# Moving the shared expert's first product into the second layer's routing stage, and slot 4's loads and the shared second product one step earlier

## The reference, cut to what matters

```
scores = sigmoid(h @ w_router)                 # 64 experts
... 8 experts of 64 per token, with gates      # group-limited top-k
routed = sum_e gate_e * (silu(h @ w_gate[e]) * (h @ w_up[e])) @ w_down[e]
shared = (silu(h @ sh_gate) * (h @ sh_up)) @ sh_down      # every token
h = layer_norm(ALPHA * h + routed + shared)
```

## Time and profile before

| | |
|---|---|
| median of 3 runs | 1616.32 us (1610.67 to 1619.49) |
| span of the profiled execution, first to last instruction | 1614.9 us |
| PE busy | 1455.4 us (90%) |
| DVE busy | 689.6 us (43%) |
| ACT busy | 355.2 us (22%) |
| POOL busy | 250.1 us (15%) |
| moved by DMA | 512.46 MB, mean 317 GB/s |
| mean granted clock of PE | 0.952 |

### The profile page before, as it was taken

How to read it: one execution, slowest core, us unless ns; L and a number is a source line. 1 busy time by engine, 2 the same in 40 slices (tenths; PEclk the granted TensorE clock), 3 DMA queues, 4 the chain that set the end, 5 groups by cost and what they waited for, 6 DMA issues and landing times. The chain is left out here.

```text
span 1614.9 us, 24656 instructions
## 1 busy us (share of the span) xinstructions
PE 1455.4 (90%) x9414; PEld 859.4 (53%) x9414; DVE 689.6 (43%) x1471; ACT 355.2 (22%) x744; POOL 250.1 (15%) x323
## 2 busy tenths in 40 slices
PE   8999888998888999797999878986999997979996
PEld 6788667887534545343454456873434342424442
DVE  3888747732433434333343349043233342323324
ACT  3766454220411111011111030122001111111111
POOL 5779515200100000000000000001000000000000
PEclk9999999899899999998999988897999998989999
DMA  7679361011999999999999973295999999999994
GB/s 272 207 190 241 137 169 54 2 53 60 393 416 420 426 422 424 423 423 424 420 425 421 406 268 110 98 401 191 362 425 424 422 425 426 422 423 422 426 423 195
DMA packets 101490, 512.46 MB, mean 317 GB/s; under 512 B 36836, under 2 KB 42020, under 8 KB 66300
## 3 DMA queue, kind: packets, MB, share of 16 engines
q1 hardware_dynamic: 91548, 481.81, 75.0%
q0 software_dynamic: 9824, 29.05, 4.7%
HBM read 508.92 MB, written 17.10 MB: 326 GB/s over the span
## 5 line engine op out<-in xcount | busy, mean ns | idle before, releaser
L1731 PE MATMUL banks<-experts,e_xgT 128*64 128x512 f32 (+1 forms) x1408 | 306.4, 608 | 1.2 <-issue 1.2
L1943 DVE TENSOR_TENSOR e_ac<-e_sl,banks 128x256 f32<-128x256 f32 x54 | 22.7, 421 | 408.3 <-ACT e_sl L1852 408.3
L280 PE MATMUL banks<-hT,dense_ring 128*128 128x272 f32 x768 | 185.4, 400 | 5.0 <-DMA dense_ring<-in_w_in 4.9
L1334 POOL DMA_INDIRECT x_xg<-rows_dram,x_idx x54 | 53.5, 991 | 853.6 <-DVE x_idx L1326 836.2
L1731 PE MATMUL banks<-dense_ring,e_xgT 128*64 128x512 f32 (+1 forms) x320 | 148.6, 619 | 39.5 <-issue 38.2
L1731 PEld LDWEIGHTS banks<-experts,e_xgT 128*64 128x64 f32 (+1 forms) x1408 | 102.4, 132 | 150.6 <-issue 150.6
L280 PEld LDWEIGHTS banks<-hT,dense_ring 128*128 128x128 f32 x768 | 147.1, 193 | 39.9 <-DMA dense_ring<-in_w_in 5.4
L1782 PE MATMUL banks<-experts,e_aT 128*64 128x512 f32 (+1 forms) x704 | 156.3, 606 | 6.2 <-DVE hT L1905 4.3
L1731 PEld LDWEIGHTS banks<-dense_ring,e_xgT 128*64 128x64 f32 (+1 forms) x320 | 41.0, 130 | 134.8 <-issue 132.7
L1852 ACT ACTIVATE e_sl<-banks 128x256 f32<-128x256 f32 x54 | 20.8, 385 | 402.3 <-PE banks L1731 402.3
L1749 PE MATMUL banks<-x_sg,e_ys 128*128 128x272 f32 x432 | 104.5, 394 | 2.8 <-ACT e_ys L1867 1.4
(11 more groups left out here) (444 smaller groups left out, 2072.6 us busy)
## 6 DMA issues: line engine op xcount, KB each, us to landing
experts<-in_moe_gate_up SPq DMA_DIRECT2D x88, 2048.0 KB, 26.8
experts<-in_moe_down SPq DMA_DIRECT2D x88, 1024.0 KB, 26.3
dense_ring<-in_moe_gate_up SPq DMA_DIRECT2D x20, 2048.0 KB, 15.2
dense_ring<-in_moe_down SPq DMA_DIRECT2D x40, 1024.0 KB, 25.2
dense_ring<-in_w_in SPq DMA_DIRECT2D x47, 512.0 KB, 4.6
e_gate_up<-in_moe_gate_up SPq DMA_DIRECT2D x10, 2048.0 KB, 19.5
x_gate_up<-in_moe_gate_up SPq DMA_DIRECT2D x10, 2048.0 KB, 19.1
dense_ring<-in_w_out SPq DMA_DIRECT2D x4, 2048.0 KB, 8.1
```

What stands on the lines that cost most here:

```text
L280: mm = pe.matmul(ps[g % 4][:, 0:T], slot[:, n % SLOTS_IN, c, :], hT[:, c, :], start=(c == 0), stop=(c == DC - 1))
L1334: pool.indirect_dma_start(out=ex["xg"][:, i % 2, :], out_offset=None, in_=mem["rows_dram"], in_offset=bass.IndirectOffsetOnAxis(ap=ex["idx ...
L1731: mm = pe.matmul(gub[e * n:(e + 1) * n, :], xgT[:, i % 2, c, e * n:(e + 1) * n], gate_up_weights(mem, j)[:, c, :], start=(c == 0), stop=(c ...
L1943: dve.tensor_tensor(ac[:], sl[:], gub[:, FF:], ALU.mult).then_inc(mul, 1)
```

## The change

`halves_ahead` goes away. In layer 1 all four halves of the shared first product, both `silu` and both products with them run in `norm_and_route`, as they already did in layer 0. SP requests slot 4's gate/up half as the first load of the expert stage in both layers (in layer 0 it was that already). In both layers `begin` moves from unit 1 to unit 0, `shared_down` and `add_shared` move from unit 2 to unit 1, and slot 4's down half is requested after them, in unit 1.

```diff
--- before.py
+++ after.py
@@ -1247,12 +1247,6 @@
     return ex
 
 
-def halves_ahead(layer):
-
-
-    return 1 if layer == DEPTH - 1 else 2 * FC
-
-
 def shared_half(pe, mem, ex, hN, bank, j, cs=range(DC)):
 
 
@@ -1370,7 +1364,7 @@
         sort = mem["sort_par"]
         key_off, number, ranks, twice, extras = (sort[:, a:b] for a, b in (
             (0, 1), (1, 2), (2, 2 + E), (2 + E, 2 + E + P), (2 + E + P, 2 + 2 * E + P)))
-        ahead, warm = halves_ahead(layer), sb("warm", [1, 1])
+        warm = sb("warm", [1, 1])
         loaded, gu_ready = mem["router_loaded"], mem["shared_gate_up_ready"]
         meaned, centred, squared, sq_summed, sd_ready, rooted, scaled, out = (sem(n) for n in (
             "meaned", "centred", "squared", "sq_summed", "deviation", "rooted", "scaled", "normed"))
@@ -1472,7 +1466,7 @@
                 pe.matmul(sort_ps[0:1, 0:E], number, at_rank[:], start=True, stop=True)
                 pe.matmul(sort_ps[0:1, E:2 * E], cm[:], at_rank[:], start=True, stop=True).then_inc(sorted_, 1)
                 shared_half(pe, mem, ex, hN, sh_ps[0], 0, range(4, DC))
-                for j in range(1, ahead):
+                for j in range(1, 2 * FC):
                     if j == 3:
                         pe.wait_ge(maxed, 1)
                     shared_half(pe, mem, ex, hN, sh_ps[j], j)
@@ -1509,7 +1503,7 @@
                 act.copy(pg[E:, 0:W], both_ps[E:, 0:W]).then_inc(placed, 1)
                 for i in range(2):
                     gates_in(act, ex, i, spread_ps[i], W)
-                for m in range(min(ahead, FC)):
+                for m in range(FC):
                     shared_silu(act, mem, ex, sh_ps, m, W)
 
             @block.vector
@@ -1605,7 +1599,7 @@
                 dve.wait_ge(ex["rows_broadcast"], 2)
                 link(dve.scalar_tensor_tensor(out=pg[0:E, 0:W], in0=maskT[:], scalar=extra[:, 0:1], in1=pg[0:E, 0:W],
                                               op0=ALU.mult, op1=ALU.add))
-                for m in range(ahead - FC):
+                for m in range(FC):
                     shared_gate(dve, mem, ex, sh_ps, m, W)
 
 
@@ -1643,8 +1637,6 @@
         summed, begun = sem("columns_summed"), sem("sums_begun")
 
 
-        sh_ps, ahead = (None, bank[7], y0b, y1b), halves_ahead(layer)
-
         spread_to = lambda i: (y0b, y1b) if i < AHEAD else (t0b, t1b)
 
         def piece(m):
@@ -1662,8 +1654,8 @@
 
             @block.sync
             def _(sp):
+                load_gate_up(sp, k, mem, layer, expert_at(sp, mem, FIXED), FIXED)
                 if not last:
-                    load_gate_up(sp, k, mem, layer, expert_at(sp, mem, FIXED), FIXED)
                     load_expert(sp, k, mem, layer, RING - 1)
                 for i, stream in enumerate(UNITS):
                     following = [j + RING for j in stream if j + RING < E]
@@ -1671,10 +1663,7 @@
                         sp.wait_ge(gu, i + 1)
                     for n, j in enumerate(following):
                         load_gate_up(sp, k, mem, layer, expert_at(sp, mem, j), j)
-                        if i == 1 and n == 1 and last:
-                            sp.wait_ge(ex["sh_gu"], 2 * FC)
-                            load_gate_up(sp, k, mem, layer, expert_at(sp, mem, FIXED), FIXED)
-                        if i == 2 and n == 1:
+                        if i == 1 and n == 1:
                             sp.wait_ge(sh_dn, PIECES)
                             load_down(sp, k, mem, layer, expert_at(sp, mem, FIXED), FIXED)
                     if following:
@@ -1811,13 +1800,7 @@
                         turn(i + 1)
                     turn_act(i)
                     if i == 1:
-                        for j in range(ahead, 2 * FC):
-                            if j == FC:
-                                pe.wait_ge(ye0, 1)
-                                pe.wait_ge(ye1, 1)
-                            shared_half(pe, mem, ex, hN, sh_ps[j], j)
                         pe.wait_ge(ex["sh_mul"], FC)
-                    if i == 2:
                         shared_down()
                     if 0 < i < N - 1:
                         combine(i - 1)
@@ -1856,9 +1839,6 @@
                     if i > 0:
                         act.wait_ge(dn, i)
                     act.copy(aT[:], atb[:, 0:FF].rearrange("p (f n) -> p f n", f=FC)).then_inc(ate, 1)
-                    if i == 1:
-                        for m in range(ahead, FC):
-                            shared_silu(act, mem, ex, sh_ps, m, W)
                     if i + AHEAD < N:
                         gates_in(act, ex, i + AHEAD, spread_to(i + AHEAD), W)
                     if last and i == N - 1:
@@ -1893,8 +1873,6 @@
                     if i > 0:
                         dve.wait_ge(addd, i * PIECES)
                     else:
-                        dve.wait_ge(begun, PIECES)
-                    if i == 1:
                         dve.wait_ge(sh_out, PIECES)
                     for m in range(PIECES):
                         dve.wait_ge(cmm, i * PIECES + m + 1)
@@ -1945,15 +1923,11 @@
                         turned_in(i + 1)
                     if i + AHEAD < N:
                         select(i + AHEAD)
-                    if i == 1:
-                        for m in range(ahead - FC if ahead > FC else 0, FC):
-                            shared_gate(dve, mem, ex, sh_ps, m, W)
-                    if i == 1:
-                        dve.wait_ge(ex["sh_gu"], 2 * FC)
+                    if i == 0:
                         for m in range(PIECES):
                             begin(m)
-                    if i == 2:
-                        dve.wait_ge(addd, PIECES)
+                    if i == 1:
+                        dve.wait_ge(begun, PIECES)
                         for m in range(PIECES):
                             add_shared(m)
                     if 0 < i < N - 1:
```

## The result

Over 20 runs of each kernel the median went from 1613.28 us to 1619.94 us: a ratio of 1.0044, 95% interval 1.0029 to 1.0059. That is 0.44% or 7 us slower, just inside the 0.5% that I had called no change, inside the range (1608 to 1621), and on the other side of zero from the forecast of -1.4 us. The three runs shown first were high for the kernel before: their median was 1616.3. That the time lies inside the range is in part luck: the base that I added the change to was 3 us high, and the change itself came out some 8 us from the forecast.

A forecast was written before the change was run, and what follows sets the result against it. The prediction took the queue of loads, not PE's matmuls, to bound the expert stages. Layer 0's +3.7 us and layer 1's -5.05 us gave -1.4 us from the median 1616.3, so 1614.9 us, range 1608 to 1621.

The forecast's parts named there:

- What bounds: Expert stages: the queue of loads at 423 to 424 GB/s sets the time; unit 17's last gate/up half ends the stage.
- All three waits on which PE was relieved: Waits for slot 4's halves, 4.22 us in layer 0, 1.25 and 2.54 in layer 1; PE then waits longer before wide units.
- Rival 2: Both expert stages: PE's order of work is the bound, so 18.1 us faster, 1598.2 us; chance 0.12 in full or one layer.
- Layer 0: Shared second product one unit earlier: request for experts 10 to 13 7.1 us later, +3.7 us, ends +2.2 and +4.6.
- Layer 1: Three halves into routing, shared second product into unit 1: -5.05 us, ends -7.05 and -3.15.
- So 8.1 us of cover stand against 10.5: Layer 1 routing: the gather wait covers 8.1 of the halves' 10.53 us, so the expert stage begins 3.9 us later.
- The 1.9 us that the clock was to give back: Layer 1, unit 0: transposes and first product at full clock after a shorter idle, cutting the 3.9 us delay to 2.0.
- Rival 1: Layer 0's queue runs dry, losing up to 7.1 us, and layer 1 doesn't pay for it: 1620.3 us, slower; chance 0.20.
- Rival 3: Neither layer's term reaches the end, for instance through queue drift: 1616.3 us; chance 0.68 together with the forecast.
- My count with 1.8 us: Layer 0, empty queue: full rate starts 1.8 us after a request, giving 3.7 us lost instead of 2.5.

The follow-up runs named there:

- first_only: Change made in layer 0 only, layer 1 as in the kernel before; ratio 1.0033 (1.0007 to 1.0059) against the kernel before.
- after_again: The changed kernel itself, run again for a second profile; ratio 1.0032 (1.0011 to 1.0052) against the kernel before.
- second_late_down: Kernel before with layer 1's halves moved into routing, slot 4's gate/up half first, shared second product left in unit 2; ratio 0.9987 (0.9971 to 1.0003).
- late_down_begin0: second_late_down with `begin` of layer 1 in unit 0; ratio 0.9990 (0.9975 to 1.0004) against the kernel before.
- before_b: The kernel before, unchanged, run for a third profile; layer 1 took 330.1 us from the first spread matmul to unit 17.
- before_again: The kernel before, unchanged, run for a second profile; layer 1 took 330.1 us from the first spread matmul to unit 17.
- pad_4: Kernel before plus 4 idle matmuls in layer 0's unit 1; no ratio given, layer 0 took 312.9 us from unit 0's transposes to unit 17.

## Why the prediction was wrong

**What bounds: right.** Everything was decided by the landing of unit 17's weights; what follows it has the same length in every profile. All three waits on which PE was relieved (4.22, 1.25 and 2.54 us) came back before the wide units: the waits there grew by 6.1 us in layer 0 and by 9.7 in layer 1, where I had said about 9 and 8. Rival 2 is out: it called for `first_only` to be faster, and it is slower.

**Layer 0: right.** Predicted: request 7.1 us later, unit 17 3.7 us later. Measured over four profiles with the change and eight without it: 49.6 against 42.8, so 6.9, and 317.95 against 314.05, so 3.9. The windows near 493 on the old scale are weak as said, but for longer, up to 499 (156 to 328 GB/s, 496 to 503 in the rows above); behind the request at 500 two are (344 and 279). So the down halves moved slower than the 424 GB/s at which I had counted them. Of the delay of the request 3.0 us did not reach unit 17, where the sum has 3.4.

**Layer 1: wrong, in the step "So 8.1 us of cover stand against 10.5".** The cover was the wait for the gather, in one execution. I said which row it was but not that its end is set by a race of two requests 0.6 us apart. In the other executions the gather lands before the barrier is over. PE then waits only the 2.3 us of the barrier, and 2.0 us of that wait stay behind the halves, so there is next to no cover. The delay of the stage was not 3.9 us less what the clock gives back, so 2.0, but 18.2 - 8.1 = 10.1 us. The other terms of the layer were nearly right: up to the request 48.6 against 53.6, so -5.0, where 3.3 + 1.3 were predicted; from there on 266.7 against 268.4, so -1.7, where 2.5 were. Sum 10.1 - 5.0 - 1.7 = +3.4 us instead of -5.05. With layer 0, +7.3 us, against 7.1 by the ratio.

Against the one execution that I predicted from, the sum would have been 333.5 - 336.3 = -2.8: still less than 5.05. The 1.9 us that the clock was to give back were only 0.7, the second term that was off; PE's idle time ahead of the transposes was 2.0 us, not 1.5. In this profile the transposes ran at the full 2.4 GHz level, as forecast (1.07 us; in after_again 1.53), but the first product behind them took 8.27 us: after 2.0 us of idle PE the granted clock fell to half, the 1.2 GHz level, when PE was already at work again. Windows of the first profile of the changed kernel; the third number from the end is the granted clock:

```profile
1127.00:1128.00 1.00, 0.64 (x6) 0.67 (x7) 0.29 (x1) 0.00 (x0) 0.00 (x0) 1.00 0.02 8
1128.50:1131.50 3.00, 3.00 (x10) 1.06 (x12) 1.69 (x5) 0.92 (x2) 0.00 (x0) 0.50 0.85 273
1132.00:1135.00 3.00, 3.00 (x18) 0.98 (x16) 0.00 (x0) 0.00 (x0) 0.89 (x1) 1.00 0.93 374
```

My nearest rows, waits of 1.25 and 4.22 us, could not tell; I looked only at the instruction right behind a wait. In rows 7 a 2.54 us wait has 0.62 us right behind it too, and the clock is 0.50 from 1183 to 1185. Against the usual execution of the kernel before, the clock gives back nothing: from unit 0's transposes to unit 1's it takes 10.1 to 10.3 us in thirteen of the profiles, with waits of 1.9 to 10.0 us before them, and 11.0 only in the first profile of before.

**Rival 1** named the sign and one of the two places, with the mechanism in layer 0 as it was, and called for over 5.05 us there. Layer 0 lost 3.9; what tipped the balance was layer 1, which it had only as a gain. Its time of 1620.3 us lies close to the 1619.94 measured, but by luck: it has 7.1 us lost in layer 0 and 3.15 gained in layer 1.

**Rival 3** (neither term reaches the end) falls with first_only, where layer 0's loss does.

**The second shared product** is the part that cost. With it left in unit 2 (second_late_down) the stretch of layer 1 is 329.8, as good as before, and layer 0 is untouched. The move into unit 1, with slot 4's down half, costs 3.9 us in layer 0 and 333.2 - 329.8 = 3.4 us in layer 1 (`begin` plays no part there, by late_down_begin0). It stands ahead of the request for experts 10 to 13, when the queue is nearly empty. Windows around the request for the down halves of experts 8 and 9 show it, in the first profile of the changed kernel (request at 1168.97):

```profile
1168.00:1169.00 1.00, 1.00 (x10) 0.29 (x12) 0.69 (x1) 0.59 (x1) 0.00 (x0) 1.00 0.65 188
1169.00:1170.00 1.00, 1.00 (x16) 0.37 (x12) 0.00 (x0) 0.00 (x0) 0.00 (x0) 1.00 0.91 250
```

and in second_late_down (request at 1156.80):

```profile
1157.00:1158.00 1.00, 1.00 (x16) 0.26 (x8) 0.00 (x0) 0.00 (x0) 0.00 (x0) 1.00 0.87 360
1158.00:1159.00 1.00, 1.00 (x12) 0.26 (x8) 0.00 (x0) 0.00 (x0) 0.00 (x0) 1.00 1.14 471
```

From 1154 to 1166 no window of second_late_down is under 360 GB/s; in the changed kernel four of the six from 1168 to 1174 are under 265 (188, 250, 160 and 262). The move of the halves alone is worth nothing: the stage starts 10.1 us later, the request then comes 53.6 - 41.7 = 11.9 us sooner, and 1.4 us of that are lost again on the way to unit 17.

The Trainium skill, DMA: Bandwidth & Descriptors, in its table of specifications, has about 0.6 us to the first byte for a transfer from SP. Here full rate came later: the four windows from 497, with the request at 497.31, stay at 213, 242, 164 and 319 GB/s. My count with 1.8 us came out at 3.7 us for layer 0, against 3.9 measured and an estimate of 2.5 by that figure.

## What to carry to other kernels

A wait that is to cover moved work should be read in several executions, and above all when what ends it is a small transfer requested within a microsecond of a large one: the wait may be there in one execution of many. When a queue of loads is the bound, ask of each step that is moved not how long it is but which request stands behind it, and how many microseconds of work the queue then still has; the same 7 us of PE work cost 3 to 4 us more ahead of unit 2's request than behind it.

## What the runs showed of the hardware

- A gather of 128 rows with 1.4 to 2.0 us of lead over 3.15 MB of weights landed 3.9 to 4.1 us after its request and held nothing up (before_b, before_again, first_only). With a lead of 1.3 us it took 4.6 us (pad_4), with 0.6 us 9.5 us, and 2.5 us behind the weights 8.3 us; PE waited 2.8, 8.1 and 10.0 us for it.
- Two down halves (2.1 MB) into a queue that had run dry, with a gather requested 2.2 or 2.3 us before them, moved at 152 to 352 GB/s for 4 to 6 us: in layer 0 of the changed kernel (497 to 503) and in layer 1 of both (1169 to 1174 after, 1158 to 1162 before), far below the 424 GB/s of a full queue. Whether the gather has a part in it was not tested. Behind a request for gate/up halves of experts 10 to 13 in layer 1 full rate was back after about 3 us (1166.29 to 1169 before, 1176.01 to 1179 after).
- The granted clock can fall after PE has gone back to work: idle 2.0 us from 1125.35, full level at 1127 to 1128, half level 1128.5 to 1131.5. The same holds behind the barrier's wait of 2.3 us in the kernel before (before_b: full at 1104 to 1105, 0.50 at 1106 to 1109).
- Work that no kernel touches drifts by 3 to 8 us from run to run (S5 mixer 156.1 to 160.9, start of layer 0's router loads 397.1 to 405.4), as much as the effect studied here.
